# Three groups of small matmuls written in another order: grams by head, M4 with M5, y by output block

## The reference

```
def step(S, inp):
    r_t, w_t, k_t, v_t, kk_t, a_t = inp
    sa = einsum('bhvk,bhk->bhv', S, -kk_t)
    S = S * w_t + sa (x) (kk_t * a_t) + v_t (x) k_t
    return S, einsum('bhvk,bhk->bhv', S, r_t)
...
y = y_f + y_b            # both directions, then a norm, a bonus term, a gate
```

## Time and profile before

| | us |
|---|---|
| median of 3 runs | 2959.98 |
| lowest, highest | 2955.38, 2965.65 |
| the profiled execution | 2955.38 |
| its span, first to last instruction | 2953.6 |
| TensorE matmuls busy | 2314.3 (78%) |
| weight loads, beside them | 1279.1 (43%) |
| VectorE, ScalarE, GpSimd busy | 688.1, 447.3, 280.4 |
| mean granted TensorE clock | 0.867 |

### The profile page before, as it was taken

How to read it: one execution, slowest core, us unless ns; L and a number is a source line. 1 busy time by engine, 2 the same in 40 slices (tenths; PEclk the granted TensorE clock), 3 DMA queues, 4 the chain that set the end, 5 groups by cost and what they waited for, 6 DMA issues and landing times.

```text
span 2953.6 us, 41742 instructions
## 1 busy us (share of the span) xinstructions
PE 2314.3 (78%) x16757; PEld 1279.1 (43%) x16757; DVE 688.1 (23%) x1246; ACT 447.3 (15%) x964; POOL 280.4 (9%) x472
## 2 busy tenths in 40 slices
PE   7999996736858577687577888879888887888874
PEld 7555663425738365574332323324232232323322
DVE  0110224536363453632310101001010010100003
ACT  1110002213233322320110100101010010100101
POOL 0000000134316061340000000000000000000000
PEclk9998887866959688697788999989899998999987
DMA  5122220000000000005159999999999999999993
GB/s 216 54 89 90 81 80 0 1 12 2 3 1 3 1 2 2 1 3 200 57 215 391 382 391 391 388 393 386 391 391 388 392 390 391 388 391 391 388 393 125
DMA packets 274125, 609.69 MB, mean 206 GB/s; under 512 B 7415, under 2 KB 41397, under 8 KB 274005
## 3 DMA queue, kind: packets, MB, share of 16 engines
q1 hardware_dynamic: 273140, 604.69, 54.9%
q0 software_dynamic: 864, 3.15, 0.3%
HBM read 605.72 MB, written 2.10 MB: 206 GB/s over the span
## 4 chain that ended last, share of the span: by engine, by line
PE 27%; DMA 21%; DVE 2%; ACT 1%; issue 1%; SPq 1%; ACTq 0%; DVEq 0%; POOL 0%; POOLq 0%
DMA expert_ring<-in_exp_w_dram 21%; PE moe_psum L1413 14%; PE moe_psum L1437 5%; PE moe_psum L1394 2%; PE moe_psum L1359 2%; PE moe_psum L1455 2%; SPq L1328 1%; ACT hidden_T L1509 1%; PE moe_psum L1371 0%; PE moe_psum L1425 0%; PE moe_psum L1351 0%; PE moe_psum L1400 0%; PE moe_psum L1398 0%; PE moe_psum L1461 0%; DVE row_bcasts L1546 0%
## 5 line engine op out<-in xcount | busy, mean ns | idle before, releaser
L1413 PE MATMUL moe_psum<-expert_ring,tokens_of_pair 128*64 128x512 f32 (+1 forms) x3072 | 683.2, 601 | 148.8 <-DMA expert_ring<-in_exp_w_dram 148.8
L1413 PEld LDWEIGHTS moe_psum<-expert_ring,tokens_of_pair 128*64 128x64 f32 x3072 | 241.5, 147 | 592.0 <-issue 451.4
L1437 PE MATMUL moe_psum<-expert_ring,hidden_T 128*64 128x512 f32 x1408 | 336.9, 620 | 64.7 <-ACT hidden_T L1509 44.9
L1611 DVE TENSOR_TENSOR hidden<-silu_out,moe_psum 64x512 f32<-64x512 f32 x96 | 61.9, 645 | 1144.0 <-ACT silu_out L1501 1144.0
L1501 ACT ACTIVATE silu_out<-moe_psum 64x512 f32<-64x512 f32 x96 | 53.2, 555 | 1125.3 <-PE moe_psum L1413 1125.3
L1437 PEld LDWEIGHTS moe_psum<-expert_ring,hidden_T 128*64 128x64 f32 x1408 | 101.4, 140 | 228.8 <-issue 172.9
L305 PE MATMUL front_psum<-xn_latent,w_ring 128*128 128x512 f32 (+1 forms) x384 | 181.0, 630 | 0.0
L267 PEld LDWEIGHTS front_psum<-silu_c,w_ring 128*128 128x128 f32 x768 | 132.5, 274 | 7.7 <-issue 7.5
L267 PE MATMUL front_psum<-silu_c,w_ring 128*128 128x2 f32 x768 | 131.8, 309 | 4.8 <-DMA w_ring<-in_mod_w_dram 4.8
L854 POOL TENSOR_TENSOR merge_a<-gram,merge_masks 64x256 f32<-64x256 f32 x144 | 111.5, 774 | 231.2 <-DVE gram L1186 214.0
L305 PEld LDWEIGHTS front_psum<-xn_latent,w_ring 128*128 128x128 f32 (+1 forms) x384 | 76.0, 200 | 93.8 <-issue 93.3
(11 more groups left out here) (363 smaller groups left out, 2331.2 us busy)
## 6 DMA issues: line engine op xcount, KB each, us to landing
expert_ring<-in_exp_w_dram SPq DMA_DIRECT2D x240, 2048.0 KB, 18.6
expert_ring<-in_exp_w_dram SPq DMA_DIRECT2D x48, 1024.0 KB, 16.7
w_ring<-in_mod_w_dram SPq DMA_DIRECT2D x12, 2048.0 KB, 8.3
w_ring<-in_w_in_dram SPq DMA_DIRECT2D x7, 2048.0 KB, 12.3
expert_ring<-in_w_out_dram SPq DMA_DIRECT2D x2, 2048.0 KB, 10.2
x_tokens<-in_x_dram POOLq DMA_DIRECT2D x4, 512.0 KB, 5.0
h_tokens<-in_x_dram SPq DMA_DIRECT2D x1, 2048.0 KB, 17.7
out_dram<-h_tokens SPq DMA_DIRECT2D x1, 2048.0 KB, 6.6
```

The lines of the kernel that those rows point to most:

```text
L1413: last = pe.matmul(ps[64 * i:64 * i + 64, HB[s_ % 2], 0:w], xs[:, k, 64 * e:64 * e + 64], slot(n)[:, k * w:(k + 1) * w], start=(k == 0), s ...
L1437: last = pe.matmul(ps[64 * hf:64 * hf + 64, YB[e], :], hidT[:, 4 * j + f, :], slot(n)[:, f * D + hf * 512:f * D + hf * 512 + 512], start=( ...
L1611: vv.tensor_tensor(hid[:, s_ % 2, 0:w], sg[:, s_ % 2, 0:w], ps[64:P, HB[s_ % 2], 0:w], ALU.mult).then_inc(sem("hid_ok"), 1)
```

## The change

The same matmuls are issued in another order at three places. First, G: head 0's three thirds, then head 1's, instead of both heads matmul by matmul; VectorE evicts in the same new order, and GpSimd and AV wait for the counts that fit it. Second, M4 and M5 alternate group by group, in `seq` and in the program. Third, y: for each chunk and head its four matmuls in a row, instead of all first products and then all second products.

```
@@ seq
-        seq += [("M4", g) for g in range(NG)] + [("M5", g) for g in range(NG)]
+        for g in range(NG):
+            seq += [("M4", g), ("M5", g)]
@@ GpSimd, level 0
-                                g.wait_ge(sem("v_G"), it * per["G"] + 6 * d + 2 * q + h + 1)
+                                g.wait_ge(sem("v_G"), it * per["G"] + 6 * d + 3 * h + q + 1)
@@ TensorE, G
-                    for q in range(3):
-                        claim("G", 6 * d + 2 * q)
-                        claim("G", 6 * d + 2 * q + 1)
+                    for i in range(6):
+                        h, q = i // 3, i % 3
+                        claim("G", 6 * d + i)
                         w = 1 if q == 0 else 2
                         for c in range(4):
                             cc = 4 * q + c
-                            for h in range(2):
-                                last = pe.matmul(at("G", 6 * d + 2 * q + h)[:, c * P:c * P + w * L], BK[d][half(h), cc, :, :],
-                                                 KR[d][half(h), cc, 0:w, :], start=True, stop=True)
-                                if c == 3:
-                                    done(last, "mm_G")
+                            last = pe.matmul(at("G", 6 * d + i)[:, c * P:c * P + w * L], BK[d][half(h), cc, :, :],
+                                             KR[d][half(h), cc, 0:w, :], start=True, stop=True)
+                        done(last, "mm_G")
@@ TensorE, AV
-                    W("v_G", per["G"], 6 * d + 2 * q + 2)
+                    W("v_G", per["G"], 6 * d + q + 1 + 3)
@@ TensorE, M4 and M5
                     done(last, "mm_M4")
-                for gi, (d, q) in enumerate(groups):
                     claim("M5", gi)
@@ TensorE, y
-                for d in range(2):
-                    for c in range(CC, CH):
-                        for h in range(2):
-                            pe.matmul(y_at(h, c), SV[d][h][:, c, :], GB[d][h][:, c, 1, :], start=(d == 0 and c == CC), stop=False)
-                for d in range(2):
-                    for c in range(CC, CH):
-                        for h in range(2):
-                            last = pe.matmul(y_at(h, c), S[d][half(h), c, :], KR[d][half(h), c, 1, :], start=False, stop=(d == 1 and c == CH - 1))
+                for c in range(CC, CH):
+                    for h in range(2):
+                        o = ps[half(h), 6, (c - CC) * L:(c - CC + 1) * L]
+                        for d in range(2):
+                            pe.matmul(o, SV[d][h][:, c, :], GB[d][h][:, c, 1, :], start=(d == 0), stop=False)
+                            last = pe.matmul(o, S[d][half(h), c, :], KR[d][half(h), c, 1, :], start=False, stop=(d == 1))
@@ VectorE, G
-                        q, h = i // 2, i % 2
+                        h, q = i // 3, i % 3
```

More of the change, by code:

```diff
@@ L761, in rwkv @@
         for d in range(2):
-            seq += [("G", 6 * d + i) for i in range(6)]
-            seq += [("KT", 3 * d + i) for i in range(3)]
+            seq += [("G", 6 * d + i) for i in range(6)] + [("KT", 3 * d + i) for i in range(3)]
         seq += [("AV", g) for g in range(NG)] + [("BT", g) for g in range(NG)] + [("XT", g) for g in range(NG)]
@@ L1001, in _ @@
                 W("v_S", per["S"], CH - 1)
-                def y_at(h, c):
-                    return ps[half(h), 6, (c - CC) * L:(c - CC + 1) * L]
-                for d in range(2):
-                    for c in range(CC, CH):
-                        for h in range(2):
-                            pe.matmul(y_at(h, c), SV[d][h][:, c, :], GB[d][h][:, c, 1, :], start=(d == 0 and c == CC), stop=False)
-                for d in range(2):
-                    for c in range(CC, CH):
-                        for h in range(2):
-                            last = pe.matmul(y_at(h, c), S[d][half(h), c, :], KR[d][half(h), c, 1, :], start=False, stop=(d == 1 and c == CH - 1))
+                for c in range(CC, CH):
[4 more added lines that the diff above has]
+                            last = pe.matmul(o, S[d][half(h), c, :], KR[d][half(h), c, 1, :], start=False, stop=(d == 1))
                 done(last, "mm_Y")
```

## The result

| us | before | after |
|---|---|---|
| median (lowest, highest), four runs of each | 2959.75 (2955.38, 2965.65) | 3073.1 (3067.4, 3076.86) |
| span of the profiled execution | 2953.6 | 3070.6 |
| mean granted clock | 0.867 | 0.851 |
| TensorE matmuls busy | 2314.3 | 2441.6 |

The ratio is 1.0375 [1.0343, 1.0407], with three further runs of the kernel after taken in (3061.03 to 3081.83): slower by 3.75%. Predicted was 3064, with a range from 3018 to 3090. The first matmul of the experts began at 1367.1 us before and at 1479.0 after, 111.9 later; from there to the end it was 1586.5 and 1591.6, 5.1 more, which is inside the scatter of either kernel. So the time was lost in the four passes.

A forecast was written before the change was run, and what follows sets the result against it. The four serial passes of the RWKV heads stage were taken as the path, with the experts starting only behind the last. Terms 3.1 + 2.2 + 19.2 + 2.2 = 26.7 us a pass, x 4 = 107, gave 3064 us, range 3018 to 3090.

The forecast's parts named there:

- y: Output stage: 64 matmuls, a tiling change at each of 63 steps, 0.38 us each at 1.2 GHz; +19.2 us a pass.
- Grams: G, one head after the other: 10.2 us a direction, hidden in direction 0, on the path in direction 1; +3.1 a pass.
- GpSimd's second wait grows by 4.6: Level 0: GpSimd's second group needs the fourth gram eviction of direction 1, not the second, so starts 4.6 us later.
- the 1.5 us that come back at a higher clock: Levels: TensorE waits less for GpSimd, so 63 records run at 2.4 GHz in half of 3.2 us; 1.5 us less.
- M4, M5 and S: M4/M5 in turns: 11 tiling steps instead of 1, +1.7, and later evictions before S, +0.5; +2.2 us a pass.
- Tail: Bonus and mean matmuls behind y: four records take 1.8 us more at 0.50, 0.4 for the rest; +2.2 a pass.
- Clock rises in y: Rival: after 13 matmuls at 1.2 GHz, y's other 51 run at 0.257 us; +12.9 a pass, 3031 us, chance 0.20.
- No drain: Rival: tiling changes leave no hole, records only serial in their column half; y +4.2 a pass, 2988 us, chance 0.10.
- Not slower: Rival: TensorE starts later matmuls on the idle half, so written order does not matter; 2952 to 2957 us, chance 0.04.
- More per matmul: Rival: common output and exposed loads; 0.5 us a matmul in y, grams 10 us more; 3096 to 3135, chance 0.06.

The follow-up runs named there:

- y_turns: Kernel before, only y changed: the two kinds of product alternate, heads in turns inside each, 31 changes of tiling; 2998.88 us, ratio 1.0104.
- y_blocks: Kernel before, only y changed: all first products, then all second ones, but one head after the other; 2975.68 us, ratio 1.0037.
- y_warm: Kernel before with y in the change's order and four idle 64 x 64 matmuls in each of 11 steps of S; 3038.31 against 2964.84 us.
- y_only: Kernel before with only the third part of the change, the new order of y; 3053.49 against 2965.0 us, ratio 1.0282.
- s_warm: Kernel before, y in its old order, with four idle 64 x 64 matmuls in each step of S; 2942.49 against 2964.84 us, ratio 0.9934.
- g_dir0: Kernel before with the new gram loops in direction 0 only, the old ones in direction 1; 2964.52 against 2962.3 us, ratio 1.0009.
- g_banks: Kernel before, only G changed: a bank's four matmuls in a row, without a partner, banks in the old order; 2965.59 us, ratio 1.0004.
- y_far: Kernel before, only y changed: one head after the other, kinds alternating, neighbours never adding to the same output; 3047.96 us, ratio 1.0273.
- y_in_chain: Kernel before with y's first products in steps 0 to 3 of S, each second product one step behind its state; 2931.42 against 2962.3 us.
- sv_gaps: Kernel before with y's first products spread over the steps of S, four matmuls in each of the first five, then two; 2939.98 against 2965.47 us.

## Why the prediction was right

**y.** Predicted 64 x 0.38 = 24.3 at 1.2 GHz; measured 0.403 each, 25.8. The mechanism (a gap at each change of tiling, no partner, the clock low all through) was right in each piece: `y_turns` shows the cost per change, `y_blocks` that one change costs little, `y_warm` the 0.257 at 2.4 GHz. The size was at the top of the stated 0.37 to 0.40, and just over it: the gap before a matmul's first record is 0.24 us, as predicted, and the second record follows after 0.16, the top of the predicted 0.13 to 0.16. That makes +1.4 a pass.

**Grams.** Predicted 10.2 us a direction and +3.1 on the path; measured 9.9 and, with AV and the levels, +4.3. The rate was right: inside one head eleven records start from 905.02 to 907.15 us, 0.213 apart, loads hidden. (The prediction's 0.104 us for both heads in turns counted records in flight; 44 start in its 5.00 us, one every 0.107, and nothing hangs on it.) The stage is shorter than 48 x 0.213 since at the change from head 0 to head 1 the last bank of one overlaps the first of the other. The text said that GpSimd's second wait grows by 4.6; it grew by 2.9 (3.65 to 6.55), because its first group also started later. What counts for the path, the second group's start behind the first gram of the pass, went from 21.79 (858.72 to 880.51) to 25.89 (883.98 to 909.87), +4.1 instead of +4.6.

The term that was wrong is the 1.5 us that come back at a higher clock:

| us behind the first gram of the pass | before, passes 1 to 4 | after, passes 1 to 4 |
|---|---|---|
| GpSimd's second group starts | 21.8 in all | 25.9 in all |
| M3 starts, the end of the levels | 95.6, 95.5, 95.7, 95.6 | 99.1, 99.1, 99.8, 101.5 |
| mean clock of the levels | 0.97, 0.94, 0.97, 0.97 | 0.97, 1.00, 0.97, 0.97 |

Behind GpSimd's +4.1 the first two passes gave back 0.6 and 0.5, the third nothing, and the last lost 1.8 more: on average +0.2 instead of -1.5. TensorE does wait less there, but in one piece, 1.45 to 1.72 us ahead of the last three groups of level 1. Behind it the clock was low as before in three of the four passes. Here the first pass, then the second:

```profile
729.47 2.45 PE L941 MATMUL rwkv_psum<-inv,merge_b 64*64 64x64 f32 x48 [1.72 <-POOL merge_b L854]
731.66 1.12 PE L941 MATMUL rwkv_psum<-prod,inv_t 64*64 64x64 f32 x16
...
930.71 0.68 PE L941 MATMUL rwkv_psum<-prod,inv_t 64*64 64x64 f32 x16
```

The 16 records took 1.12 us in passes 1, 3 and 4 and 0.68 in pass 2. There the clock did what was forecast, and yet the rest of level 1, from 930.71 to 938.73, took 8.0 us where it took 7.9 before (901.14 to 909.02): the profile has idle time in it that it puts down to nothing it shows ("issue"), 1.45 us instead of 0.45. What sets these gaps is open. That the levels as a stage are 2.1, 2.8, 1.7 and 0 us shorter is no sign of the clock. TensorE comes to them 5.6 us and more later and GpSimd's products only 4.1, so it waits less for GpSimd there: 1.5 to 1.7 us in one piece, where it was 3.1 to 3.2 in four.

**M4, M5 and S.** Predicted +2.2, measured +2.3: ten added changes at (9.05 - 7.58)/10 = 0.147 us (0.17 was taken), and 0.5 for VectorE's evictions, both as worked out. S took 0.3 us more on average. In the second pass its steps grew from 0.99 to 1.23 us after the second step, before after the fifth, less a first step that was 0.13 shorter.

**Tail.** Predicted +2.2, measured +2.3.

**Not predicted.** In two passes the low-rank products ran in part at the higher clock; here the second:

```profile
859.91 1.55 PE L893 MATMUL rwkv_psum<-rwkv_in,w_up_pair 64*128 64x512 f32 x4
861.31 1.45 PE L893 MATMUL rwkv_psum<-rwkv_in,a_up_pair 64*128 64x512 f32 x4
```

In the third pass the first of these took 2.93 us at 1.2 GHz. That gave back 4.4 and 2.5 us, 1.7 a pass on average. It is luck of the clock and no effect of the change that these runs could show: `y_only`, with the same y and the same tail, has it in none of its four passes, `s_warm` in two and `g_dir0` in one. This luck is also why the sum of the stages came out so near: +4.3 + 2.3 + 20.6 + 2.3 - 1.7 = 27.8 a pass, 26.7 predicted, with +2.8 from y, grams, S and tail against -1.7. Why the clock is high there in some passes and not in others is open; no run here varied that alone.

**Rivals.** "Clock rises in y": out, by the 0.50 over 25 us and by `y_warm`. "No drain": out, by `y_blocks` and `y_turns`. "Not slower", with later matmuls started on the idle half: partly true of G, as `g_banks` shows at the border of two banks, and here only at the change from head 0 to head 1, too late to help the first evictions. "More per matmul" by the common output: out, by `y_far`, and by exposed loads: out, by the 9.9 us of the grams.

The Trainium skill, TensorEngine Tiling (Array Packing), Key Properties, says that a change of tiling mode drains TensorE. The runs agree and give the size for these fp32 tiles: a matmul or a pair between two changes takes 0.40 to 0.41 us at 1.2 GHz (0.257 for one at 2.4), where turns of one tiling start a matmul every 0.058 us at 2.4 GHz (without the records in flight). The Trainium skill, TensorE: Matmul & The Clock Gate, What overlaps and what doesn't, says that a weight load overlaps matmuls in flight only when its row group differs. By an estimate with the prediction's 0.2 us for a load the serial grams would then take some 20 us a direction; they took 9.9, with loads busy 7.56 of 7.80 us beside them.

## What to carry to other kernels

Group small matmuls by the tiling of the array, and let neighbours take different halves: at 2.4 GHz a matmul alone between two changes of tiling took as long as four to five in steady turns (0.257 and 0.058 us), and one alternating loop of 64 matmuls became five times as long. Put independent matmuls into the gaps of a dependent chain, at the chain's own tiling where it can be had; here they filled the wait and also kept the clock up, through all of S in `y_in_chain` and for nine of its steps in `sv_gaps`. Before counting what a slower stage costs, look who waits for it: twice the time for the grams cost nothing in direction 0 and 4 us in direction 1.

## What the runs showed of the hardware

The busy time of the page doesn't tell which clock is granted: 25 us of isolated matmuls, busy throughout, stayed at 1.2 GHz, and the chain of `s_warm`, busy 8.50 of 12.00 us, stayed at 2.4. One half alone stayed at 1.2 GHz in the grams and rose in `y_blocks`. Idle matmuls in the gaps of S made this kernel 0.66% faster. Matmuls written one bank after the other on different halves overlap at the border without any turn inside (6.7 us instead of 9.9 for 48 records). And in the grams one fp32 record with a 128-column load takes 0.21 us at 1.2 GHz in one half whether it moves 64 columns (the first eight records of a head) or 128 (the sixteen behind them).
